# A hybrid decoder layer on one core: the RWKV chunk inverses of two token blocks, side by side and in 64x64 tiles

## What is computed

```
x += 0.5 * SwiGLU_1(RMSNorm(x))
h  = RMSNorm(x);  P = h @ w_in        # attention | RWKV-7 | short convolution
x += concat(attention, rwkv, conv) @ w_out
x += 0.5 * SwiGLU_2(RMSNorm(x))
```

```
S_t = S_{t-1} diag(w_t) + (S_{t-1} a_t) b_t^T + v_t k_t^T ;   y_t = S_t r_t
```

## Time and profile before

| | us |
|---|---|
| median of three runs | 2255.14 |
| lowest, highest | 2253.01, 2265.03 |
| profiled execution | 2254.84 |
| its span | 2253.2 |
| TensorE busy | 2165.5 (96%) |
| VectorE busy | 1219.6 (54%) |
| ScalarE busy | 883.2 (39%) |
| GpSimd busy | 209.7 (9%) |

### The profile page before, as it was taken

The page is one execution under the profiler, slowest core; times in us unless marked ns, Lnnn a source line. Parts: engine busy times, 40 slices in busy tenths (PEclk is TensorE's granted clock), DMA queues, the critical chain, the costliest instruction groups (busy, mean ns, idle before and its releaser), DMA issues.

```text
span 2253.2 us, 44718 instructions
## 1 busy us (share of the span) xinstructions
PE 2165.5 (96%) x18348; PEld 2136.8 (95%) x18348; DVE 1219.6 (54%) x1279; ACT 883.2 (39%) x1011; POOL 209.7 (9%) x173
## 2 busy tenths in 40 slices
PE   6999999999999999999985899999999999999997
PEld 5999999999999999999965898999999999999997
DVE  5555555555444554789756455555555555544442
ACT  4443444444434444343242243444444444434332
POOL 3000000000000000143018710100000000000000
PEclk9999999999999999999977799999999999999999
DMA  4655555555555566678620013555655555556553
GB/s 154 187 182 181 180 183 178 180 182 175 187 175 175 181 194 185 192 218 255 216 64 6 30 39 102 179 181 178 185 177 185 178 182 181 177 168 198 185 170 103
DMA packets 359028, 373.43 MB, mean 166 GB/s; under 512 B 13329, under 2 KB 351797, under 8 KB 358742
## 3 DMA queue, kind: packets, MB, share of 16 engines
q1 hardware_dynamic: 349280, 348.17, 49.6%
q0 software_dynamic: 5920, 17.48, 3.1%
q10 hardware_dynamic: 3742, 6.52, 0.9%
HBM read 366.82 MB, written 5.32 MB: 165 GB/s over the span
## 4 chain that ended last, share of the span: by engine, by line
PE 90%; DVE 5%; DMA 2%; ACT 1%; issue 1%; POOL 0%; ACTq 0%; SPq 0%; POOLq 0%; DVEq 0%
PE ps L298 27%; PE ps L300 27%; PE ps L299 27%; PE ps L1511 3%; DMA raw<-in_w_in_dram 2%; DVE wL L285 1%; PE ps L1057 1%; PE ps L1393 1%; DVE xL L332 0%; DMA vrowa<-in_rwkv_mu_dram 0%; ACT wH L279 0%; PE ps L1625 0%; PE ps L1384 0%; PE ps L1634 0%; PE ps L1398 0%
## 5 line engine op out<-in xcount | busy, mean ns | idle before, releaser
L285 DVE TENSOR_TENSOR wL<-raw,wH 128x1024 fp32r<-128x1024 f32 (+1 forms) x676 | 827.8, 1230 | 863.4 <-ACT wH L279 863.1
L279 ACT ACTIVATE wH<-raw 128x1024 fp32r<-128x1024 f32 (+1 forms) x676 | 700.1, 1038 | 1012.1 <-PE ps L300 945.8
L298 PE MATMUL ps<-xH,wH 128*128 128x264 f32 x3616 | 1031.6, 285 | 12.8 <-DVE wL L285 12.7
L300 PE MATMUL ps<-xH,wL 128*128 128x264 f32 x3616 | 1029.4, 285 | 0.0
L299 PE MATMUL ps<-xL,wH 128*128 128x264 f32 x3616 | 1029.3, 285 | 0.0
L298 PEld LDWEIGHTS ps<-xH,wH 128*128 128x128 f32 x3616 | 683.6, 189 | 14.8 <-issue 14.1
L300 PEld LDWEIGHTS ps<-xH,wL 128*128 128x128 f32 x3616 | 683.3, 189 | 0.0
L299 PEld LDWEIGHTS ps<-xL,wH 128*128 128x128 f32 x3616 | 682.7, 189 | 0.2
L298 PE MATMUL ps<-hH,wH 128*128 128x264 f32 x1408 | 402.4, 286 | 0.0
L300 PE MATMUL ps<-hH,wL 128*128 128x264 f32 x1408 | 401.4, 285 | 0.0
L299 PE MATMUL ps<-hL,wH 128*128 128x264 f32 x1408 | 401.2, 285 | 0.0
(11 more groups left out here) (332 smaller groups left out, 1363.1 us busy)
## 6 DMA issues: line engine op xcount, KB each, us to landing
raw<-in_ffn_w_gate_dram SPq DMA_DIRECT2D x176, 512.0 KB, 3.5
raw<-in_ffn_w_up_dram SPq DMA_DIRECT2D x176, 512.0 KB, 3.5
raw<-in_ffn_w_down_dram SPq DMA_DIRECT2D x128, 512.0 KB, 3.4
raw<-in_w_in_dram SPq DMA_DIRECT2D x100, 512.0 KB, 5.0
raw<-in_ffn_w_down_dram SPq DMA_DIRECT2D x64, 384.0 KB, 3.0
raw<-in_w_out_dram SPq DMA_DIRECT2D x32, 512.0 KB, 3.9
kb<-in_cache_swa_k_dram POOLq DMA_DIRECT2D x24, 256.0 KB, 6.5
vb<-in_cache_swa_v_dram ACTq DMA_DIRECT2D x24, 256.0 KB, 5.7
```

The source lines that it names most:

```text
L279: nc.scalar.activation(wH[:, k % RING, 0:nk, :], raw[:, k % RING, 0:nk, :], ACT.Copy).then_inc(S("head_made"), 1)
L285: nc.vector.tensor_tensor(wL[:, k % RING, 0:nk, :], raw[:, k % RING, 0:nk, :], wH[:, k % RING, 0:nk, :].bitcast(F32), ALU.subtract).then_i ...
L298: nc.tensor.matmul(out, wH[:, k % RING, q, cols], high, start=a, stop=False)
L300: last = nc.tensor.matmul(out, wL[:, k % RING, q, cols], high, start=False, stop=b)
```

## The change

- The inverses of both blocks run in one pass (`pe_inverse`, `dve_inverse`): at each level Q of block 0, Q of block 1, Z, Z, X, X. Each has its own tensors (`Zq`, `Xq`, `Aq`, `Qq`, and `Aak`, `Arb`, `Ark`, `tokv`, `tokb`, `tokk` twice).
- The level products are 64x64x64, 24 for a block, addressed by row half and column half (`place`). Q and X are stored with heads and chunks exchanged: rows by head parity, columns by chunk. The block matrices, their clears on GpSimd and ScalarE's `blocks` are gone, as are the neighbour's columns.
- ScalarE copies each Q out in one piece of 128x768. VectorE takes Z and X in one piece each. Six of the twelve Grams stand in front of the levels, the other six in the first three levels.
- ScalarE writes the identities, in `act_gates`; the value transposes stand in `pe_gates`. Those of b and k come at the last level and behind it.
- The four chunk steps follow in a row. Block 1's own products stand in step 1, and ScalarE copies them. In the state, the sum with the old one is written in PSUM. y's copy waits for the state's part too.
- The group norm of the first 128 columns is cut in two halves of three tiles (parts 0 and 1), placed in steps 2 and 3 and behind them; part 2 is the rest. The heads and tails of w_out's first chunks move behind part 2's centring, tails 2 and 3 behind the last split.
- GpSimd halves the samples' sums once (`halve`) and VectorE sums the remaining 32 (`dve_sample_sums`) and makes `ycat`.
- `zoT` and `so` move to another place; their DMAs get a semaphore of their own, for which ScalarE waits at the root of the third norm.

The core of the diff:

```diff
-        for m in (Abd, Xbd, Qbd):
-            if m is Abd:
-                pool.wait_ge(S("decayed"), 4)
-            nc.gpsimd.memset(m[:], 0.0).then_inc(S("blocks_cleared"), 1)
+        pool.wait_ge(S("decayed"), 4)
...
-            while w > 1:
-                step(g.tensor_tensor(S2[:, :, 0:w], S2[:, :, 0:w], S2[:, :, w:2 * w], ALU.add))
-                w //= 2
-            step(g.tensor_tensor(out, S2[:, :, 0], S2[:, :, 1], ALU.add))
+            g.tensor_tensor(S2[:, :, 0:w], S2[:, :, 0:w], S2[:, :, w:2 * w], ALU.add).then_inc(S("sums_halved"), 1)
...
+        for m in (Zq[0], Zq[1], Xq[1]):
+            identity(m)
+        for n in range(2):
+            stage_tokens(act, tokv[n], n, (6, 4)[n])
+        act.wait_ge(S("decayed"), 3)
+        identity(Xq[0])
...
+    GRAMS = (("Z", 0, 0), ("X", 0, 4), ("A", 0, 6), ("Z", 1, 2), ("X", 1, 4), ("A", 1, 6),
+             ("Aak", 0, 4), ("Arb", 0, 6), ("Ark", 0, 4), ("Aak", 1, 6), ("Arb", 1, 4), ("Ark", 1, 6))
+    LATE_GRAMS = ((6, 7), (8, 9), (10, 11))
+    def every():
+        return ((i, b, cp) for i in range(RT) for b in range(2) for cp in range(2))
...
+    def pe_level_q(pe, lv, n):
+        if lv:
+            pe.wait_ge(S("z_level"), 2 * lv - 1 + n)
+            pe.wait_ge(S("x_level"), 2 * lv - 1 + n)
...
+        for i, b, cp in every():
+            last = nc.tensor.matmul(place(HALF[b], 2 * n + cp, i), Aq[n][HALF[cp], slot(b, i), :],
+                                    Zq[n][HALF[cp], slot(b, i), :], start=True, stop=True)
+    def pe_level_z(pe, lv, n):
+        pe.wait_ge(S("level_q_out"), 2 * lv + n + 1)
+        for i, b, cp in every():
+            last = nc.tensor.matmul(place(HALF[cp], 2 * n + b, i), Xq[n][HALF[b], slot(cp, i), :],
+                                    Qq[n][HALF[b], slot(cp, i), :], start=True, stop=True)
+    def pe_level_x(pe, lv, n):
+        pe.wait_ge(S("z_level"), 2 * lv + n + 1)
+        for i, b, cp in every():
+            last = nc.tensor.matmul(place(HALF[b], 2 * n + cp, i), Qq[n][HALF[b], slot(cp, i), :],
+                                    Xq[n][HALF[b], slot(cp, i), :], start=True, stop=True)
...
+        for lv in range(LEVELS):
+            for n in range(2):
+                pe_level_q(pe, lv, n)
+            if lv == 4:
+                pe.wait_ge(S("grams_out"), gram("Arb", 1))
+                turn_tokens(pe, bT, 0, 4)
+                pe.wait_ge(S("grams_out"), gram("Ark", 1))
+                turn_tokens(pe, pkr, 0, 6)
+            for n in range(2):
+                pe_level_z(pe, lv, n)
+            if lv < len(LATE_GRAMS):
+                for k in LATE_GRAMS[lv]:
+                    pe.wait_ge(S("grams_out"), k - 1)
+                    pe_gram(pe, k)
+            if lv < 4:
+                for n in range(2):
+                    pe_level_x(pe, lv, n)
...
+        for lv in range(LEVELS):
+            for n in range(2):
+                act.wait_ge(S("level_q"), 2 * lv + n + 1)
+                cp(split(Qq[n]), region(2 * n), ACT.Copy).then_inc(S("level_q_out"), 1)
...
+        act_group_squares(act, 2)
+        act.wait_ge(S("sample_state_out"), 16)
+        act.wait_ge(S("sums_halved"), 2)
+        for k in range(2):
+            head(act, CK, OUT, OUT_PER, 0, k)
+        act_group_root(act, 2)
+        for k in range(2, 4):
+            head(act, CK, OUT, OUT_PER, 0, k)
+        act_rwkv_head(act, 0)
...
+    def dve_sample_sums(dve, k):
+        dve.wait_ge(S("sums_halved"), k)
+        nc.vector.tensor_reduce(smal[:, 0:C], S2[:, :, 0:C // 2], AX.X, ALU.add).then_inc(S("sample_sums"), 1)
...
+        dve_group_scaled(dve, 0)
+        dve_sample_sums(dve, 2)
+        dve.wait_ge(S("sample_sums"), 2)
+        for a in range(2):
+            v.tensor_scalar(ycat[:, a, :], smal[:, 0:C], cgat[:, 48 + a:49 + a], None, ALU.mult
+                            ).then_inc(S("sample_y"), 1)
+        dve_group_scaled(dve, 1)
...
+        dve_group_centre(dve, 2)
+        for k in range(2):
+            tail(dve, CK, OUT, OUT_PER, 0, k)
+        dve_group_scale(dve, 2)
+        dve_group_scaled(dve, 2)
+        dve.wait_ge(S("group_scaled"), 3)
         dve_rwkv_tail(dve, 0)
         group_gate(dve, v, 1, lambda instrs: linked(instrs, dve))
         dve_rwkv_tail(dve, 1)
+        for k in range(2, 4):
+            tail(dve, CK, OUT, OUT_PER, 0, k)
```

More of the change, by code:

```diff
@@ L1345, in pool_rwkv @@
         step(g.tensor_tensor(S2[:], S1[:], key(4), ALU.mult))
[L1346 to L1349, removed]
+        halve()
         pool.wait_ge(S("sample_state_out"), 16)
@@ L1404, in pe_gates, with turn_tokens @@
         last.then_inc(S("vectors_turned"), 1)
+        pe.wait_ge(S("vectors_staged"), 1)
+        turn_tokens(pe, pvr, 0, 6)
+        pe.wait_ge(S("decayed"), 1)
+        turn_tokens(pe, pvr, 1, 4)
+    def turn_tokens(pe, src, half, first):
+        for j in range(RT):
+            last = nc.tensor.transpose(ps[:, first + j // 3, j % 3 * P:j % 3 * P + P],
+                                       src[:, j, half * P:half * P + P], ident)
+        last.then_inc(S("tokens_turned"), 1)
     def act_gates(act):
@@ new lines, in bank, with place, chunk, pe_gram @@
+    def bank(first, b):
+        return ps[:, first + b, 0:RT * C].rearrange("p (h c) -> p h c", c=C)
+    def place(rows, b, i):
+        return ps[rows, b, i * C:i * C + C]
+    def chunk(n):
+        return slice(n * C, n * C + C)
+    def every():
+        return ((i, b, cp) for i in range(RT) for b in range(2) for cp in range(2))
+    def pe_gram(pe, k):
+        name, n, first = GRAMS[k]
+        left, right = dict(Z=(bT, aT), X=(aT, bT), A=(aT, bT), Aak=(pkr, aT), Arb=(bT, pr), Ark=(pkr, pr))[name]
+        for i, b, cp in every():
+            c = chunk(2 * n + cp)
+            out = place(HALF[b], first + cp, i) if name == "X" else place(HALF[cp], first + b, i)
+            last = nc.tensor.matmul(out, left[HALF[b], i, c], right[HALF[b], i, c], start=True, stop=True)
+        last.then_inc(S("grams_made"), 1)
@@ L1700, in pe_group_sums, with tiles @@
+    def tiles(m, part):
+        cols, js, _ = GROUP[part]
+        return m[:, js, cols].rearrange("p (b j) c -> p b j c", j=3)
+    def pe_group_sums(pe, part):
+        cols, js, _ = GROUP[part]
+        if part == 1:
+            pe.wait_ge(S("group_centred"), 1)
+        for j in range(js.start, js.stop):
+            k = j - js.start
+            last = nc.tensor.matmul(group_bank(part)[:, k // 3, k % 3, :], blk, pvr[:, j, cols], start=True, stop=True)
         last.then_inc(S("group_sums"), 1)
@@ L1711, in pe_group_spread @@
     def pe_group_spread(pe, part):
-        cols, _ = GROUP[part]
-        pe.wait_ge(S("head_scale"), part + 2)
-        for j in range(RT):
-            last = nc.tensor.matmul(group_bank(part)[:, j // 3, j % 3, :], hs[:, j * P:j * P + P], hn[:, cols],
+        cols, js, _ = GROUP[part]
+        pe.wait_ge(S("head_scale"), 2 + part // 2)
+        if part == 1:
+            pe.wait_ge(S("group_scaled"), 1)
+        for j in range(js.start, js.stop):
+            k = j - js.start
+            last = nc.tensor.matmul(group_bank(part)[:, k // 3, k % 3, :], hs[:, j * P:j * P + P], hn[:, cols],
                                     start=True, stop=True)
@@ L1758, in act_rwkv_head @@
     def act_rwkv_head(act, part):
-        cols, _ = GROUP[part]
+        cols = COLS[part]
         act.wait_ge(S("rwkv_made"), part + 1)
@@ L1804, in act_chunks, with dve_gram @@
         act_rwkv_head(act, 1)
+    def dve_gram(dve, k):
+        v = nc.vector
+        name, n, first = GRAMS[k]
+        dve.wait_ge(S("grams_made"), k + 1)
+        if name == "Z":
+            ins = v.copy_predicated(split(Zq[n]), mask(4, True), region(first))
+        elif name == "X":
+            ins = v.copy_predicated(split(Xq[n]), mask(5, True), region(first))
+        else:
+            m, out = dict(A=(SL, Aq), Aak=(SU, Aak), Arb=(IU, Arb), Ark=(IU, Ark))[name]
+            ins = v.tensor_tensor(split(out[n]), region(first), mask(m), ALU.mult)
+        ins.then_inc(S("grams_out"), 1)
```

534 lines of the change are left out of this document (237 added, 297 removed).

## The result

| | before | after |
|---|---|---|
| median, us | 2254.07 (4 runs) | 2193.12 (4 runs) |
| lowest, highest | 2251.99, 2265.03 | 2191.89, 2205.53 |
| profiled execution | 2254.84 | 2205.53 |
| its span | 2253.2 | 2203.7 |

The ratio is 0.9729, 95% interval 0.9689 to 0.977: 61 us less. The prediction was 2189.1 in a range of 2170 to 2222. The intervals are as wide as they are because the executions of before fall in two groups, some 2249 to 2256 and 2260 to 2268.

The account below looks back on a forecast made before the run. The RWKV stage's chain of waits, 182.6 us, was taken as what bounds the stretch. Terms 6.4+40.8+42+7.6+20.1 = 116.9, so 65.7 us off 2254.84: 2189.1 us, range 2170 to 2222.

Parts of the forecast that it names:

- Set-up, 6.4 us: From the last decay product to the first Q product: Gram Z, three evacuations, a Gram; 4.9 us full clock, 7.8 half.
- Levels, 40.8 us: Both blocks' interleaved level products with late Grams: 39.0 us at full clock, 57 at half, taken nine tenths towards full.
- TensorE has 5.8 us of work: In a level: TensorE's work for both blocks, against a 6.8 us chain per block, so the other block fits beside it.
- allowance for the clock (1.8): In the levels: clock taken nine tenths towards full, giving 40.8 us where full clock gives 39.0.
- X at two quarters' pace: In each level: X uses only the two diagonal quarters, 48 instructions in 1.44 us at full clock, 2.58 at half.
- Chunk steps, 42 us between 33.2 and 51: Four chunk steps in a row with own products and group sums: 33.2 us full clock, 51 half, middle taken.
- To the sample columns, 7.6: From last state product to sample columns: VectorE's reciprocal, state, scaling, sample sums, placing, then a product and hand-overs, 7.6 us.
- Group norm, gate, first product, 20.1: Last columns' group norm to w_out's first RWKV product: 16.1 us before, plus 1.2, 1.2 and 1.6, together 20.1.
- the tails' part of it, 2.4: In the group norm term: +1.2 for heads and tails ahead of root and reciprocal, +1.2 for tail 2.
- serial quarters: Rival in the levels: quarters don't overlap, 2.54 us for each Gram and level set, 2245 us; chance 0.03.
- The rival of a clock at half: Through the whole RWKV stage: the granted clock stays at half, giving 2218 us; chance 0.10.
- my two grounds against it: Against half clock: the Grams of 1201 to 1205 are small tiles too, and 1206 to 1208 has clock 1.00.

Follow-up runs that it names:

- half the instructions: Changed kernel with 128-column products in Grams and level sets, half as many, odd tiles getting copies of even tiles' inverses (output not the layer's): 2177.22 us, 0.9632 of before.
- again: The changed kernel once more, no edit, for a second profile: 2191.63 us, profiled execution 2193.44 us.
- the light fill: Early tails kernel plus added 64-row products, 4 in the first chunk step, 2 in the second, none later: 2187.82 us, 0.9709 of before.
- the early tails: Changed kernel with w_out's first four heads ahead of ScalarE's squares, three VectorE tails ahead of the group norm's centring, one behind: 2189.22 us.

## Why the prediction was right, and where it wasn't

- *Set-up, 6.4 us; 7.1 and 7.6.* Right in what goes: the identities and value transposes vanish behind the decay products. But the chain there is TensorE alone, where I had three evacuations and two Grams. All six early Grams stand ahead of Q, and in after they take 1.34, 2.21, 0.71, 0.75, 1.34 and 0.71 us. The first two ran at half clock, and the second and fifth are X Grams, which like X sets have two quarters only. I had not priced these Grams so, nor the six in a row. It isn't the instruction supply: with half the instructions it took 7.2 us. After's clock, then, in the kernel with half the instructions, the first Grams (chain) and the first Q instruction (timeline):

```profile
1192.00:1196.00 4.00, 3.26 (x85) 3.26 (x86) 1.70 (x2) 0.00 (x0) 3.14 (x1) 0.50 0.02 4
```

```profile
1194.72 4.17 PE ps L1590 x48
1201.95 0.28 PE L1603 MATMUL ps<-Zq,Aq 64*64 64x128 f32 x2
```

- *Levels, 40.8 us; 48.1 and 48.0, at clock 1.00.* The one term clearly mis-sized. The step that failed is "TensorE has 5.8 us of work" in a level: I took the pace of single sets, 15 and 30 ns. Over a stretch it gets a matmul instruction in 28 ns: 288 in a level with X sets, 384 with late Grams, so 8.1 and 10.8 us, against 8.0 and 10.9 to 11.4 measured. It cost 11.7 us (48.1 against the 36.4 with half the instructions); 4.4 of these my sum had already, by its allowance for the clock (1.8) and by laying the levels out too long (39.0 against 36.4).
- *X at two quarters' pace*: right (1.44 us and a last one's 0.25 priced, 1.68 measured where it ran freely). By the supply's pace it cost little, which wasn't tested apart. The Trainium skill, TensorEngine Tiling (Array Packing), Gotcha 1: PSUM Pressure, says that different row tiles can't access one PSUM bank at the same time; by my estimate that meant an X set of 2.54 us, as its two row halves write the same two banks. The trace's 1.68 disagrees, and so do the products of the state with r, which write one bank from both halves: 21 instructions in 0.86 us in again. The copies' throughput didn't bind: VectorE was busy 25.9 of 48 us.
- *Chunk steps, 42 us between 33.2 and 51*: 48.7, 37.3, 32.7 with the light fill, and 31.7 with half the instructions, at full clock. The ends were about right, and 42 is up to 9 us off; the executions differ by just this.
- *To the sample columns, 7.6; 9.3.* I left out the spread product of the second part, 1.59 us, which TensorE runs ahead of the sample columns (L1780).
- *Group norm, gate, first product, 20.1; 21.6 and 20.1.* Right, and the tails' part of it, 2.4, is what the early tails took off (2.6).
- *Rivals.* The half clock in the levels and serial quarters didn't come. The rival of a clock at half held for the first Grams and the chunk steps. Of my two grounds against it one was empty: at 1206 to 1208, where I read 1.00, TensorE executed nothing.

The sum was 116.9 against 122.3 in a typical execution. It landed 4 us off the median because the levels (+7.2: the supply's 11.7 less the 4.4 of slack in my layout), the set-up (+1.2) and the sample columns (+1.7) met a better chunk clock (-4.7). So the total is right in part by luck: the mechanism of the levels was missing, and the clock, which I had only bracketed, made up for it. Of the gain, the runs put 18.8 us on the interleaving and 10.5 on the identities, each in its own stage (alone, the identities brought the kernel's median 2.7 us); the rest, tiles, blocks and tails together, was not taken apart.

## What to carry to other kernels

Count TensorE's instructions over the whole stretch, weight loads too, and not only the pace of a set: tiles so small that a set outruns its supply gain only up to the supply. A faster part in a chain is worth what its first reader gets sooner. And where a stretch of small products ran at full clock in one kernel, it may not in the next: the identities' 10.5 us were mostly lost that way. In the profiles 1.7 us of added work went with full clock, where the longer stretch at half cost 11; that the whole kernel gains by it is not shown.

## What the runs showed of the hardware

- TensorE's instructions came in packets of 16,384 bytes for each 128 matmul instructions with their loads, in the levels one in 3.7 us on average, so one matmul instruction in 28 ns; demand above that made it stand still, mostly about a microsecond (0.9 to 1.8), at fixed numbers of the instruction stream, until 1.2 to 1.6 us behind a packet's landing. What sets that rate (a packet takes 0.9 to 1.3 us) wasn't tried.
- The granted clock in one and the same kernel differed by execution: in the chunk steps half for 41 us or for 14, with 11 us between the lengths. It stayed at full with added products over 64 rows as with those over 128.
- Products that wrote one PSUM bank from both row halves in turn (state with r) kept two quarters' pace: 21 instructions in 0.86 us.
